# Attention and cell of a two-block model: steps half a unit apart, moving means begun behind their own tile, a narrower gate unit

## Chip, cores and metric

One NeuronCore of one Trainium2 chip runs the kernel. The metric is device time in microseconds. Five engines work beside each other, each through its own queue in program order: TensorE (PE), VectorE (DVE), ScalarE (ACT), GpSimd (POOL) and SyncE (SP), which issues the weight loads. They wait for each other by semaphores alone.

## What is computed

512 tokens of width 1024 in fp32 pass through two blocks. The first is a hybrid mixer (a state-space scan in four groups, and a pooling branch) with a feed-forward net. The second is a token mixer of sliding-window attention and a matrix-memory cell (mLSTM), again with a feed-forward net. What the change touches:

```
def causal_multiscale_pool(u, pool_w, pool_scale):
    ...
    for gi, win in enumerate(POOL_WINDOWS):            # 2, 4, 8, 16
        ...
        mean = (csg[:, 1:] - start) / jnp.minimum(count, float(win))
        outs.append(mean - u32[..., gi * gw:(gi + 1) * gw])

def token_mixer(h, w_in, ...):
    proj = h @ w_in
    qk_ml, v_ml, o_ml, gates, q_at, kv_at = jnp.split(proj, cuts, axis=-1)
    qk_ml = jax.nn.silu(causal_dwconv(qk_ml, ml_conv_w, ml_conv_b))
    ...
    h_ml = rms_norm(mlstm_chunkwise(q_ml, k_ml, v_ml, i_pre, logf), ml_norm_g) * jax.nn.sigmoid(o_ml)
    o_at = sliding_window_attention(rope(q_at), rope(k_at), v_at, attn_sinks)     # softmax with a sink
    return jnp.concatenate([h_ml, rms_norm(o_at, attn_norm_g)], axis=-1) @ w_out
```

## The kernel before

**Units.** Every weight matrix is cut into units of at most 2048 columns per partition (`plan_units`, L72). For each unit SP loads `raw` (L512), ACT rounds it to `w_hi` (`split_hi`, L1012, the activation at L1018) and POOL forms the rest, `w_lo` (`split_lo`, L553, four pieces at L561). PE then makes three products of each pair of tiles (L713 for outputs by token, L717 by channel): w_hi with the rounded activations, with their rest, and w_lo. Weights have two slots: ACT rounds the weights of the next unit at the start of a unit in its own order, so whatever ACT does at the end of the unit before stands ahead of them, and POOL and PE wait for them.

**Half units.** PE runs a unit in two halves (`project`, part 0 and 1), 24 matmuls of 512 columns each in most units. `plan_steps` (L196) gives each unit three lists of small steps: `before`, `mid` (after the first half) and `end` (after the second). Every engine walks the same lists and does its share of each step. ACT and DVE evict the tiles of a half unit ahead of its steps. `by_rank` (L191) sorts the steps of a list: those named first in `rank` (L267) come first, the rest keep their order. A slot below is one such list; slot 2n is the middle of unit n and 2n+1 its end.

**Banks.** PSUM has four banks for projections (`main`) and four for small steps, A to D. `BANKS_OF` (L275) fixes which step uses which, in order: att_scores and att_turn both use B and C, att_out D, rope_q and k_turn A, ml_scores B and C, ml_out D, B, A, C, A, C. PE may write a bank only once its last reader has freed it.

**Pooling branch.** Units U (four, two tiles each) give the pooled channels, which ACT copies to `xs_tok` (L1046). `window(t)` (DVE L1715, ACT L1242) makes tile t's moving mean by doublings, one for a window of 2 and four for 16 (L1729, L1730), corrects the first 16 tokens (L1733, L1734), scales and subtracts (L1735); ACT rounds it (L1244) and DVE forms the rest (L1738). Window 0 stands at the end of the last U unit and waits for all of its four last tiles; the others follow a half unit apart, through Y0, Y1 and the first two GS units. Units Y0, Y1 are the last group's branch, evicted by DVE (L1446), GS are gates, evicted by ACT (tanh, L1052) and DVE (L1451). DVE also adds a piece of the modulation in each (`ada_piece`, L1556).

**Second block's mixer.** Units in order: KV, QA0, QA1, GA (gates of the cell), QK (four, convolved), V0, V1, O0, O1, WO. A convolved tile (`convolve`) costs ACT L1028, then DVE three L1391, for which ACT waits, then ACT's tanh L1030; DVE's L1416 comes with the next tile. The attention runs in eight rounds q (four blocks of queries by two key heads):

- att_scores(q): PE L859, DVE L1746 to L1753 (scale, mask, maximum, sink), ACT L1262 and L1263 (exponentials)
- att_turn(q): PE transposes the probabilities (L872), ACT copies them out (L1271)
- att_out(q): PE L885, DVE L1758 to L1762; each second one also has the norm of the block, on ACT (L1283), POOL (L610, L611) and DVE (L1769)

att_scores(q) stands at the end of unit GA+q, att_turn(q) in the middle of the next and att_out(q) at its end: one round in a unit. GA has two tiles of 128 columns, 4 of them used in each, evicted with their bias by L1520. At its end stand rope_q 2 and 3 (PE L843, ACT L1254, both bank A) and ml_gates, which is one step: DVE sets rows to zero, ACT makes log-sigmoids, DVE scans them (L1780 to L1789), ACT takes exponentials (L1292 to L1295). ml_columns (PE L893, L897) needs those. k_turn(hd) needs a scaling by ACT (L1299), then PE L906 and ACT's copy L1303. The cell runs in four chunks: ml_scores(c) (PE L913, L917; DVE L1811, ACT L1309, DVE L1818 to L1824) and ml_out(c) (PE L927, L937, L943; DVE L1832 to L1856; POOL L615, L616; DVE L1867), from the end of V1 to before WO. The join multiplies by the output gate (L1874, four of them ahead of the first transposition), transposes (PE L950, L955), scales (DVE L1881), rounds (ACT L1316) and forms the rest (POOL L622); WO waits for all of it.

Of the kernel before, what the change touches and what calls it, by code (L numbers as in the profile page):

```python
# [9 lines left out]
ALU = mybir.AluOpType  # L10
# [61 lines left out]
def plan_units():  # L72
# [28 lines left out]
    u += [Unit("GA", "w_in_2", 0, KD, [(GATES2, MH, P - MH), (GATES2 + MH, MH, P - MH)], "h")]  # L101
# [94 lines left out]
def plan_steps(units):  # L196
# [39 lines left out]
    n = at["U"][3]  # L236
    for t in range(KD):
        (end, mid)[t % 2][n + (t + 1) // 2].append(("window", t))
# [28 lines left out]
    rank = ["silu", "b_turn", "ssd_out", "ssd_scores", "xs_turn", "ssd_turn"]  # L267
# [22 lines left out]
def build(nc, stream, w_ada, w_ada2, x_in, params_in, consts_in, out):  # L290
# [22 lines left out]
    with ExitStack() as ctx:  # L313
# [51 lines left out]
        with ExitStack() as s5:  # L365
# [16 lines left out]
            att = alloc(s5, "att", [32])  # L382
# [11 lines left out]
        def sem(name):  # L394
# [27 lines left out]
            ).split()]  # L422
        seg_rhs = [seg_first[:, c, :, :] for c in range(TC - 1)] + [seg_last[:, :, :]]
# [121 lines left out]
        def _(pool):  # L545
# [59 lines left out]
            def att_out(q, n):  # L605
                if q % 2 == 0:
                    return
                i = q // 2
                pool.wait_ge(at_sq, i + 1)
                link(nc.gpsimd.tensor_scalar(att[:, 26:27], att[:, 25:26], 1.0 / (AH * AD), RMS_EPS, ALU.mult, ALU.add))  # L610
                nc.gpsimd.tensor_tensor(att[:, 27:28], att[:, 26:27], small[:, 63:64], ALU.pow).then_inc(at_rs, 1)  # L611
# [13 lines left out]
            stages = {"seg_rows": seg_rows_, "ssd_scores": ssd_scores, "ssd_out": ssd_out, "att_out": att_out,  # L625
# [24 lines left out]
        def _(pe):  # L650
# [212 lines left out]
            def att_turn(q, n):  # L863
                i = q // 2
                pe.wait_ge(sm_exp, q + 1)
                for b in range(2):
                    bank, full = take(("att_turn", q), b)
                    for j in range(2):
                        for r in range(2):
                            if i == 0 and r == 0:  # L870
                                continue
                            ins = nc.tensor.transpose(bank[:, 2 * P * j + P * r:2 * P * j + P * (r + 1)],  # L872
                                                      prob[:, 2 * b + j, chunk(r)], ident)
                    ins.then_inc(full, 1)

            def att_out_(q, n):
# [4 lines left out]
                for j in range(4):  # L881
                    for r in range(2):
                        if i == 0 and r == 0:
                            continue
                        ins = nc.tensor.matmul(bank[:, AD * j:AD * (j + 1)], prob_t[:, j, r, :],  # L885
# [35 lines left out]
            def ml_out_(c, n):  # L921
# [8 lines left out]
                pe.wait_ge(v_ready, TC)  # L930
# [56 lines left out]
        def _(act):  # L987
# [44 lines left out]
            def evict(u, t):  # L1032
# [56 lines left out]
                elif u.name == "O1":  # L1089
                    bank, free = tile(j)  # L1090
                    link(run_act(og[:, t, :], bank[:, :], ACT.Tanh, scale=0.5))
# [166 lines left out]
            def att_scores(q, n):  # L1258
                ks = slice(P, 2 * P) if q < 2 else slice(0, 2 * P)
                act.wait_ge(sm_max, q + 1)  # L1260
                for j in range(4):
                    run_act(prob[:, j, ks], prob[:, j, ks], ACT.Exp, bias=att[:, 8 + j:9 + j], accum_out=att[:, 12 + j:13 + j])  # L1262
                run_act(att[:, 16:20], att[:, 16:20], ACT.Exp).then_inc(sm_exp, 1)  # L1263

            def att_turn(q, n):
                rs_ = 1 if q < 2 else 0
                if q:
                    read_by_pe(("att_out", q - 1), 0)
                for b in range(2):
                    bank, free = full(("att_turn", q), b)  # L1270
                    link(run_act(prob_t[:, 2 * b:2 * b + 2, rs_:2, :],  # L1271
# [4 lines left out]
            def att_out(q, n):  # L1276
                if q % 2:
                    i = q // 2
                    act.wait_ge(at_raw, q + 1)
                    read_by_pe(("ml_columns", 0), 0)  # L1280
                    if i:
                        act.wait_ge(at_rs, i)
# [722 lines left out]
```

## Time and profile before

| | |
|---|---|
| median of 3 runs | 1898.7 us (1897.71 to 1898.96) |
| the profiled execution | 1899.32 us, span 1897.5 us |
| mean granted clock of PE | 0.943 |
| PE matmul busy | 1704.9 us, 90% |
| PE weight loads busy | 1368.1 us, 72% |
| DVE / ACT / POOL busy | 874.3 / 637.6 / 799.2 us (46 / 34 / 42%) |
| chain that ended last, by engine | PE 70%, DVE 14%, ACT 6%, POOL 5%, issue 3% |
| HBM | 191.80 MB read, 102 GB/s over the span |

Times inside the profile count from the start of its span. Busy times say how much an engine did, and not who held up whom; for that the waits and the timelines of a stretch are read. A granted clock of 1.00 is 2.4 GHz, 0.50 is 1.2 GHz, and values between are a mean over a stretch at the two.

### The profile page before, as it was taken

Reading aid. Unit: us, or ns where it says so; the run is one execution under the profiler, and the core shown is the slowest. Engines: PE = TensorE matmul, PEld = TensorE weight load, DVE = VectorE, ACT = ScalarE, POOL = GpSimd, SP = SyncE. Lnnn points to the kernel's source line nnn. Section 1 sums busy time; section 2 is a strip of 40 time slices with the busy share of each in tenths; the row PEclk is TensorE's granted clock in tenths of the full one; section 3 lists DMA queues with packets and bytes.
Section 4 is the critical chain, followed back from the end, with each engine's and each line's share of the span. In section 5 each row is a group of like instructions: output and inputs, shape, how many; then the busy total and the mean of one; then the engine's idle time right before and its main releaser. Section 6 shows DMA issues by size and latency. Waiting matters only on the chain.

```text
span 1897.5 us, 20659 instructions
## 1 busy us (share of the span) xinstructions
PE 1704.9 (90%) x7616; PEld 1368.1 (72%) x7616; DVE 874.3 (46%) x1153; ACT 637.6 (34%) x827; POOL 799.2 (42%) x639
## 2 busy tenths in 40 slices
PE   3988999999979997999999987788869699999995
PEld 1666788787857885788888856667757377888884
DVE  5536455544484344543343455552561655203424
ACT  3534434343223223431143222443222434324331
POOL 1263555455444553455445523232134145444441
PEclk7988999999989998999999988897879799999998
DMA  8111112122324541345534531111002033232221
GB/s 308 45 67 45 67 67 89 67 89 89 122 82 166 185 177 68 131 142 185 186 136 153 178 133 48 64 50 62 23 23 71 22 130 126 76 120 89 84 92 58
DMA packets 35234, 195.22 MB, mean 103 GB/s; under 512 B 3904, under 2 KB 4032, under 8 KB 19648
## 3 DMA queue, kind: packets, MB, share of 16 engines
q1 hardware_dynamic: 23616, 151.96, 22.3%
q10 hardware_dynamic: 11520, 41.95, 6.4%
q8 instruction: 62, 1.02, 0.2%
q14 instruction: 36, 0.29, 0.0%
HBM read 191.80 MB, written 2.10 MB: 102 GB/s over the span
## 4 chain that ended last, share of the span: by engine, by line
PE 70%; DVE 14%; ACT 6%; POOL 5%; issue 3%; DMA 1%; DVEq 0%; SPq 0%; ACTq 0%; POOLq 0%
PE main L717 54%; PE main L713 8%; POOL w_lo L561 4%; ACT w_hi L1018 2%; DVE rstd L1591 1%; PE auxB L741 1%; DVE tmp L1391 1%; DVE h_lo L1621 1%; DVE tmp L1531 1%; PE auxD L820 1%; DMA ada_first<-w_ada 1%; DVE x L1606 1%; DVE ysum L1605 1%; DVE tmp L1730 1%; PE auxD L733 1%
## 5 line engine op out<-in xcount | busy, mean ns | idle before, releaser
L561 POOL TENSOR_TENSOR w_lo<-raw,w_hi 128x512 fp32r<-128x512 f32 (+1 forms) x525 | 707.6, 1379 | 903.8 <-ACT w_hi L1018 903.6
L717 PE MATMUL main<-h_hi,w_hi 128*128 128x512 f32 (+1 forms) x1144 | 460.4, 402 | 44.5 <-POOL w_lo L561 16.9
L717 PE MATMUL main<-h_lo,w_hi 128*128 128x512 f32 (+1 forms) x1144 | 451.9, 395 | 0.0
L717 PE MATMUL main<-h_hi,w_lo 128*128 128x512 f32 (+1 forms) x1144 | 451.7, 395 | 0.0
L1018 ACT ACTIVATE w_hi<-raw 128x2048 fp32r<-128x2048 f32 (+3 forms) x136 | 249.3, 1833 | 261.2 <-PE main L717 222.4
L717 PEld LDWEIGHTS main<-h_hi,w_hi 128*128 128x128 f32 (+1 forms) x1144 | 218.0, 191 | 110.1 <-issue 27.7
L717 PEld LDWEIGHTS main<-h_hi,w_lo 128*128 128x128 f32 (+1 forms) x1144 | 217.5, 190 | 48.3 <-issue 1.0
L717 PEld LDWEIGHTS main<-h_lo,w_hi 128*128 128x128 f32 (+1 forms) x1144 | 218.5, 191 | 42.9
L1531 DVE SCALAR_TENSOR_TENSOR tmp<-main,par,tmp 128x511 f32<-128x511 f32 x88 | 65.9, 749 | 176.3 <-ACT tmp L1107 174.7
L1556 DVE SCALAR_TENSOR_TENSOR ada_acc<-ada_raw,cs,ada_acc 128x1024 f32<-128x1024 f32 x70 | 115.3, 1648 | 29.2 <-DMA ada_raw<-w_ada 21.3
L713 PE MATMUL main<-w_hi,h_hi 128*128 128x512 f32 (+1 forms) x256 | 105.6, 412 | 19.8 <-POOL w_lo L561 10.2
L713 PE MATMUL main<-w_hi,h_lo 128*128 128x512 f32 (+1 forms) x256 | 101.8, 397 | 0.0
L713 PE MATMUL main<-w_lo,h_hi 128*128 128x512 f32 (+1 forms) x256 | 101.5, 397 | 0.0
L717 PE MATMUL main<-f_hi,w_hi 128*128 128x512 f32 x256 | 100.0, 391 | 0.0
L717 PE MATMUL main<-f_hi,w_lo 128*128 128x512 f32 x256 | 99.7, 389 | 0.0
L717 PE MATMUL main<-f_lo,w_hi 128*128 128x512 f32 x256 | 99.6, 389 | 0.0
L1391 DVE SCALAR_TENSOR_TENSOR tmp<-main,half,tmp 128x511 f32<-128x511 f32 (+2 forms) x96 | 71.9, 748 | 48.0 <-ACT tmp L1028 45.5
L713 PEld LDWEIGHTS main<-w_hi,h_hi 128*128 128x128 f32 x256 | 52.0, 203 | 33.9 <-POOL w_lo L561 11.0
L717 PE MATMUL main<-g_hi,w_hi 128*128 128x512 f32 x176 | 68.7, 390 | 0.8 <-POOL w_lo L561 0.8
L717 PE MATMUL main<-g_lo,w_hi 128*128 128x512 f32 x176 | 68.5, 389 | 0.0
L717 PE MATMUL main<-g_hi,w_lo 128*128 128x512 f32 x176 | 68.5, 389 | 0.0
L1485 DVE TENSOR_TENSOR tmp<-tmp 128x512 f32<-128x512 f32 x32 | 24.7, 771 | 93.5 <-ACT f_hi L1079 93.5
(329 smaller groups left out, 2390.8 us busy)
## 6 DMA issues: line engine op xcount, KB each, us to landing
raw<-stream SPq DMA_DIRECT2D x119, 1024.0 KB, 4.9
ada_raw<-w_ada ACTq DMA_DIRECT2D x80, 512.0 KB, 4.2
ada_first<-w_ada SPq DMA_DIRECT2D x16, 512.0 KB, 6.8
raw<-stream SPq DMA_DIRECT2D x8, 768.0 KB, 4.1
raw<-stream SPq DMA_DIRECT2D x8, 640.0 KB, 3.8
x<-x_in SPq DMA_DIRECT2D x2, 2048.0 KB, 10.6
out<-x SPq DMA_DIRECT2D x8, 256.0 KB, 2.0
con<-consts SPq DMA_DIRECT2D x1, 486.0 KB, 3.7
```

What stands on the lines that cost most here:

```text
L561: ins = nc.gpsimd.tensor_tensor(w_lo[:, s, a:b], raw[:, s, a:b], w_hi[:, s, a:b], ALU.subtract)
L713: ins = nc.tensor.matmul(bank[:, 0:u.cols], a[:, ka_, chunk(t)], w[:, k, :], start=start, stop=stop)
L717: ins = nc.tensor.matmul(bank[0:n, :], w[:, k, col:col + n], a[:, ka_, :], start=start, stop=stop)
L733: ins = nc.tensor.matmul(aux["D"][:, :], ones, tmp[:, k % 2, :], start=(k == 0), stop=(k == KD - 1))
L741: ins = nc.tensor.matmul(bank[:, t:t + 1], acc[:, chunk(t)], ones[:, 0:1], start=True, stop=True)
L820: ins = nc.tensor.matmul(bank[:, HD * k:HD * (k + 1)], decay[:, k, :], xdt[:, 0, HD * k:HD * (k + 1)], start=True, stop=True)
L1018: run_act(w_hi[:, s, 0:k], raw[:, s, 0:k], ACT.Copy).then_inc(hi_done, 1)
L1391: ins = stt(acc[:, d:SEQ], bank[:, 0:SEQ - d], w[:, 3 - d:4 - d], acc[:, d:SEQ], ALU.mult, ALU.add)
L1485: link(tt(tmp[:, 2 + n % 2, :], tmp[:, n % 2, :], tmp[:, n % 2, :], ALU.mult))
L1531: link(stt(acc[:, d:SEQ], bank[:, 0:SEQ - d], wt, acc[:, d:SEQ], ALU.mult, ALU.add))
L1556: link(stt(acc, src, c, acc, ALU.mult, ALU.add))
L1591: link(nc.vector.reciprocal(rstd[:, :], rstd[:, :]))
```

## The change

- Windows of the pooling branch: window t moves to slot 2·U[2]+t, and DVE waits for its own tile alone.
- GA packs both gates into one tile of 36 columns; DVE copies the two groups of rows out, frees the bank and adds the biases after.
- ml_gates is cut into three steps (ml_gates, ml_scan, ml_exp) at the end of GA, the middle of QK0 and its end.
- Attention: one round in each half unit from the middle of QK0: scores in slot s, turn in s+2, output in s+3. `prob` and `prob_t` get a second buffer each, which lies in `og`, and `att` has four slots. The block norm becomes the steps att_square and att_norm.
- k_turn starts half a unit earlier; ml_scores and ml_out stand half a unit apart, from the middle of V1; v_ready is awaited chunk by chunk.
- The join multiplies each chunk by its gate just before that chunk is transposed.
- `rank` is longer.

```diff
-    u += [Unit("GA", "w_in_2", 0, KD, [(GATES2, MH, P - MH), (GATES2 + MH, MH, P - MH)], "h")]
+    u += [Unit("GA", "w_in_2", 0, KD, [(GATES2, MH, 32 - MH), (GATES2 + MH, MH, 0)], "h")]
...
-    n = at["U"][3]
     for t in range(KD):
-        (end, mid)[t % 2][n + (t + 1) // 2].append(("window", t))
+        slot(2 * at["U"][2] + t).append(("window", t))
...
-    mid[at["GA"][0]] += [("rope_q", 0), ("rope_q", 1)]
-    end[at["GA"][0]] += [("rope_q", 2), ("rope_q", 3), ("ml_gates", 0)]
+    end[at["GA"][0]] += [("rope_q", 0), ("rope_q", 1), ("ml_gates", 0)]
+    mid[at["QK"][0]] += [("rope_q", 2), ("rope_q", 3), ("ml_scan", 0)]
+    end[at["QK"][0]] += [("ml_exp", 0)]
     mid[at["QK"][1]] += [("ml_columns", 0)]
     for hd in range(MH):
-        (end, mid)[hd % 2][at["QK"][3] + (hd + 1) // 2].append(("k_turn", hd))
-    n = at["GA"][0]
+        slot(2 * at["QK"][3] + hd).append(("k_turn", hd))
+    first = 2 * at["QK"][0]
     for q in range(2 * TC):
-        end[n + q + 1].append(("att_out", q))
-    for q in range(2 * TC):
-        mid[n + q + 1].append(("att_turn", q))
-        end[n + q].append(("att_scores", q))
-    end[at["V1"][0]] += [("ml_scores", 0)]
-    mid[at["O0"][0]] += [("ml_out", 0), ("ml_scores", 1)]
-    end[at["O0"][0]] += [("ml_out", 1), ("ml_scores", 2)]
-    mid[at["O1"][0]] += [("ml_out", 2), ("ml_scores", 3)]
-    before[at["WO"][0]] += [("ml_out", 3)] + [("join", c) for c in range(TC)]
+        slot(first + q).append(("att_scores", q))
+        slot(first + q + 2).append(("att_turn", q))
+        slot(first + q + 3).append(("att_out", q))
+    for i in range(TC):
+        slot(first + 2 * i + 5).append(("att_square", i))
+        slot(first + 2 * i + 6).append(("att_norm", i))
+    for c in range(TC):
+        slot(2 * at["V1"][0] + c).append(("ml_scores", c))
+        slot(2 * at["V1"][0] + c + 1).append(("ml_out", c))
+    before[at["WO"][0]] += [("join", c) for c in range(TC)]
...
-    rank = ["silu", "b_turn", "ssd_out", "ssd_scores", "xs_turn", "ssd_turn"]
+    rank = ["silu", "b_turn", "ssd_out", "ssd_scores", "xs_turn", "ssd_turn", "rope_q", "ml_columns", "att_turn", "att_out",
+            "att_scores", "k_turn", "ml_out", "ml_scores"]
...
+        probs = [prob[:, :, :], og[:, 0:2, :].rearrange("p a (j k) -> p (a j) k", k=2 * P)]
+        probs_t = [prob_t[:, :, :, :], og[:, 2:4, :].rearrange("p a (j r k) -> p (a j) r k", r=2, k=P)]
...
-                pe.wait_ge(v_ready, TC)
+                pe.wait_ge(v_ready, c + 1)
...
             def att_turn(q, n):
                 rs_ = 1 if q < 2 else 0
-                if q:
-                    read_by_pe(("att_out", q - 1), 0)
+                if q >= 2:
+                    read_by_pe(("att_out", q - 2), 0)
...
-                    link(ts((row_i, row_f)[t], bank[0:MH, :], pc("gate_b", t, t + 1)[0:MH, :], None, ALU.add))
+                    nc.vector.tensor_copy(row_i, bank[0:MH, :])
+                    link(nc.vector.tensor_copy(row_f, bank[32:32 + MH, :]))
                     dve.sem_inc(free, 1)
+                    ts(row_i, row_i, pc("gate_b", 0, 1)[0:MH, :], None, ALU.add)
+                    link(ts(row_f, row_f, pc("gate_b", 1, 2)[0:MH, :], None, ALU.add))
...
             def window(t, n):
...
-                if t == 0:
-
-                    j = units[unit_at["U"][3]].job0 + 1
-                    for b in range(4):
-                        dve.wait_ge(main_free[(j - b) % 4], (j - b) // 4 + 1)
-                else:
+                j = units[unit_at["U"][t // 2]].job0 + t % 2
+                dve.wait_ge(main_free[j % 4], j // 4 + 1)
+                if t:
                     dve.wait_ge(pl_lo, t)
...
-                    for k in range(TC):
-                        stt(hm[:, k, :], og[:, k, :], 1.0, hm[:, k, :], ALU.add, ALU.mult).then_inc(ml_out, 1)
+                stt(hm[:, c, :], og[:, c, :], 1.0, hm[:, c, :], ALU.add, ALU.mult).then_inc(ml_out, 1)
```

## Rows read from the trace of the kernel before

**Rows 1.** Windows: us, PE, PEld, DVE, ACT, POOL busy (x), PEclk, DMA share, GB/s.
```profile
528.80:579.90 51.10, 38.03 (x148) 30.41 (x147) 38.41 (x60) 11.10 (x13) 22.34 (x14) 0.87 0.27 93
...
1203.20:1291.40 88.20, 69.55 (x314) 56.67 (x313) 45.00 (x90) 39.74 (x80) 21.69 (x20) 0.86 0.14 48
1291.40:1403.40 112.00, 96.10 (x486) 79.56 (x486) 49.73 (x115) 32.78 (x70) 25.88 (x26) 0.90 0.11 38
```

**Rows 2.** Waits of PE, 505 to 580 us: total, times, longest.
```profile
PE main L717 <- POOL w_lo L561: 13.1, 3, 5.7
```

**Rows 3.** Waits of PE, 1187 to 1426 us.
```profile
PE auxB L872 <- ACT att L1263: 13.5, 3, 8.9
PE auxA L906 <- ACTq L1300: 9.0, 3, 5.0
```

**Rows 4.** Timeline of POOL near 525 us: start, length, instruction, idle before.
```profile
526.70 6.55 POOL L561 TENSOR_TENSOR w_lo<-raw,w_hi 128x512 fp32r<-128x512 f32 x4 [9.76 <-ACT w_hi L1018]
```

**Rows 5.** Timeline of DVE, windows 0 and 1 (507 to 519 us).
```profile
507.08 0.15 DVE L1729 COPY tmp<-xs_tok 128x1 f32<-128x1 f32 x1 [16.52 <-ACT xs_tok L1046]
507.15 0.68 DVE L1730 TENSOR_TENSOR tmp<-xs_tok 128x511 f32<-128x511 f32 x1
...
509.59 0.69 DVE L1738 TENSOR_TENSOR p_lo<-tmp,p_hi 128x512 fp32r<-128x512 f32 x1 [0.76 <-ACT p_hi L1244]
...
512.72 1.81 DVE L1730 TENSOR_TENSOR tmp<-xs_tok 128x511 f32<-128x511 f32 x1
...
518.31 0.69 DVE L1738 TENSOR_TENSOR p_lo<-tmp,p_hi 128x512 fp32r<-128x512 f32 x1 [0.76 <-ACT p_hi L1244]
```

**Rows 6.** Timeline of POOL, w_lo of QK0.
```profile
1189.73 5.15 POOL L561 TENSOR_TENSOR w_lo<-raw,w_hi 128x512 fp32r<-128x512 f32 x4 [5.75 <-ACT w_hi L1018]
```

**Rows 7.** Timeline of DVE, ml_gates' scans up to the first scores.
```profile
1207.74 0.68 DVE L1780 SCALAR_TENSOR_TENSOR k_tok<-k_tok,v 4x512 f32<-4x512 f32 x1 [4.73 <-ACT v L1290]
...
1213.79 0.40 DVE L1746 SCALAR_TENSOR_TENSOR prob<-auxB,con 128x256 f32<-128x256 f32 x1
```

**Rows 8.** Timeline of ACT, 1251 to 1261 us: exponentials, a convolution, the turned copies.
```profile
1251.48 0.51 ACT L1262 ACTIVATE prob<-prob,att 128x256 f32<-128x256 f32 x1 [4.99 <-DVE att L1753]
...
1253.55 1.90 ACT L1018 ACTIVATE w_hi<-raw 128x2048 fp32r<-128x2048 f32 x1
1255.35 0.76 ACT L1028 ACTIVATE tmp<-main,half 128x512 f32<-128x512 f32 x1
1258.55 0.63 ACT L1030 ACTIVATE tmp<-tmp 128x512 f32<-128x512 f32 x1 [2.44 <-DVEq L1395]
...
1259.86 0.60 ACT L1271 ACTIVATE prob_t<-auxC 128x512 f32<-128x512 f32 x1 [0.18 <-ACT prob_t L1271]
```

**Rows 9.** Chain that ended last, 1250 to 1560 us: two half units and WO.
```profile
1300.35 5.49 PE main L713 x24
...
1337.86 7.55 PE main L713 x24
...
1424.95 46.45 PE main L717 x192
```

**Rows 10.** Score matmuls of one bank: timeline near 1264, groups of 1282 to 1292.
```profile
1264.20 1.02 PE L859 MATMUL auxC<-ka,qa 64*128 64x256 f32 x4
...
L859 PE MATMUL auxC<-ka,qa 64*128 64x256 f32 x4 | 1.9, 631 | 0.0
```

**Rows 11.** Timeline of DVE, one round's scores: first and last instruction.
```profile
1248.07 0.69 DVE L1746 SCALAR_TENSOR_TENSOR prob<-auxB,con 128x512 f32<-128x512 f32 x1 [0.15 <-DVE qa L1769]
...
1251.29 0.15 DVE L1753 TENSOR_TENSOR att<-par,att 128x4 f32<-128x4 f32 x1
```

**Rows 12.** Timeline of DVE, ml_out and ml_scores of one slot: first and last.
```profile
1383.27 0.43 DVE L1832 TENSOR_TENSOR tmp<-auxA,qcol 128x258 f32<-128x258 f32 x1 [3.48 <-PE auxD L937]
...
1395.06 0.70 DVE L1824 TENSOR_TENSOR tmp<-v,qcol 128x516 f32<-128x516 f32 x1 [0.25 <-DVE tmp L1819]
```

**Rows 13.** Groups of POOL, 1414 to 1425 us.
```profile
L622 POOL TENSOR_TENSOR h_lo<-tmp,h_hi 128x512 fp32r<-128x512 f32 x8 | 9.9, 1273 | 4.8 <-ACT h_hi L1316 4.8
```

More of the change, by code:

```diff
@@ L381, in build @@
             dec = alloc(s5, "dec", [MH * TC])
-            att = alloc(s5, "att", [32])
+            att = alloc(s5, "att", [4, 32])
             decb = alloc(s5, "decb", [MH * TC])
@@ L603, in ssd_out, with att_square @@
                 nc.gpsimd.tensor_tensor(ss[:, 2:3], ss[:, 1:2], small[:, 63:64], ALU.pow).then_inc(y_rs, 1)
[L605 to L608, printed above, removed]
+            def att_square(i, n):
+                st = att[:, i % 4, :]
                 pool.wait_ge(at_sq, i + 1)
[L610 to L611 removed]
+                link(nc.gpsimd.tensor_scalar(st[:, 26:27], st[:, 25:26], 1.0 / (AH * AD), RMS_EPS, ALU.mult, ALU.add))
+                nc.gpsimd.tensor_tensor(st[:, 27:28], st[:, 26:27], small[:, 63:64], ALU.pow).then_inc(at_rs, 1)
             def ml_out_(c, n):
@@ L1090, in evict @@
                     bank, free = tile(j)
+                    if t == 0:
+                        read_by_pe(("att_out", 2 * TC - 1), 0)
                     link(run_act(og[:, t, :], bank[:, :], ACT.Tanh, scale=0.5))
@@ L1274, in att_turn, with att_square @@
                     act.sem_inc(pt_ready, 1)
[L1276 to L1282, printed above, removed]
-                    run_act(quant[:, :], qa[:, i, :, :].rearrange("p t d -> p (t d)"), ACT.Square,
-                            accum_out=att[:, 25:26]).then_inc(at_sq, 1)
+            def att_square(i, n):
+                act.wait_ge(at_raw, 2 * i + 2)
+                read_by_pe(("ml_columns", 0), 0)
+                run_act(quant[:, :], qa[:, i, :, :].rearrange("p t d -> p (t d)"), ACT.Square,
+                        accum_out=att[:, i % 4, 25:26]).then_inc(at_sq, 1)
             def ml_gates(i, n):
@@ L1290, in ml_gates, with ml_exp @@
                 run_act(row_e, row_e, ACT.Ln, bias=ones[0:MH, 0:1]).then_inc(mg_e, 1)
+            def ml_exp(i, n):
                 act.wait_ge(mg_x, 2)
@@ L1320, in _ @@
                       "b_turn": b_turn, "ssd_scores": ssd_scores, "ssd_norm": ssd_norm, "ssd_out": ssd_out, "ssd_turn": ssd_turn, "window": window,
-                      "rope_k": rope_k, "rope_q": rope_q, "att_scores": att_scores, "att_turn": att_turn, "att_out": att_out,
-                      "ml_gates": ml_gates, "k_turn": k_turn, "ml_scores": ml_scores, "join": join}
+                      "rope_k": rope_k, "rope_q": rope_q, "att_scores": att_scores, "att_turn": att_turn, "att_square": att_square,
+                      "ml_gates": ml_gates, "ml_exp": ml_exp, "k_turn": k_turn, "ml_scores": ml_scores, "join": join}
             count = {}
@@ L1742, in att_scores @@
                 ks = slice(P, 2 * P) if q < 2 else slice(0, 2 * P)
-                kn = ks.stop - ks.start
+                pr, st = probs[q % 2], att[:, q % 4, :]
+                if q >= 2:
+                    full(("att_turn", q - 2), 1)
                 for b in range(2):
                     bank, free = full(("att_scores", q), b)
-                    ins = stt(prob[:, 2 * b:2 * b + 2, ks], bank[:, :].rearrange("p (j k) -> p j k", j=2)[:, :, ks],
+                    ins = stt(pr[:, 2 * b:2 * b + 2, ks], bank[:, :].rearrange("p (j k) -> p j k", j=2)[:, :, ks],
                               float(AD) ** -0.5, each(cc("band", ks.start, ks.stop), 2), ALU.mult, ALU.add)
@@ L1777, in ml_gates, with ml_scan @@
                 dve.sem_inc(mg_x, 1)
+            def ml_scan(i, n):
+                scan = nc.vector.tensor_tensor_scan
                 dve.wait_ge(mg_e, 1)
@@ L1889, in _ @@
                       "ssd_scores": ssd_scores, "ssd_out": ssd_out, "ssd_turn": ssd_turn, "window": window,
-                      "att_scores": att_scores, "att_out": att_out, "ml_gates": ml_gates, "ml_columns": ml_columns,
+                      "att_scores": att_scores, "att_out": att_out, "att_norm": att_norm, "ml_gates": ml_gates,
+                      "ml_scan": ml_scan, "ml_columns": ml_columns,
                       "ml_scores": ml_scores, "ml_out": ml_out_, "join": join}
```

41 lines of the change are left out of this document (21 added, 20 removed).

## The prediction

> **What bounds the kernel now.** I read the tables by stretch first. In the windows of the pooling branch PE was busy 38.03 of 51.1 us; in the attention stretch (1203.2 to 1291.4) 69.55 of 88.2, in the stretch of the cell 96.10 of 112.0, at mean granted clocks of 0.87, 0.86 and 0.90 [rows 1]. Elsewhere PE is nearly full, so what the change can win lies in these stretches. The waits of PE say who ends them: in the first, w_lo of the next unit's weights, 13.1 us in 3 waits [rows 2]; in the others, L872 on the exponentials of ACT (13.5 us, the longest 8.9) and L906 on k_turn's scaling (9.0 us in 3) [rows 3]. The timelines of ACT and DVE then show why these are late: both run in program order, and each waits inside a step for the other.
>
> The bound that a measurement can tell from no change is 0.2%, 3.8 us. I sum against the profiled run (1899.32 us, of which 1.8 us lie outside its 1897.5 us span) and take the difference off the median of 1898.7, 0.6 us lower.
>
> **Windows of the pooling branch.** No instruction is added; three of four waits before the first window go, and windows 0 to 7 move three half units earlier. What hurts now: ACT's p_hi copy waits for each window, and w_hi of the next unit stands behind it. w_lo of GS0, held by it, ran from 526.70 to 533.25, and GS0 began then instead of at 528.8, where its stretch begins [rows 1, 4]. A window with two taps took 3.1 us on DVE (507.08 to 510.2), and 6.3 (512.7 to 519.0) where POOL ran w_lo beside it [rows 5]. Each doubling adds what the first one took, 507.08 to 507.83, 0.8 us: 3.1, 3.9, 4.7, 5.5 alone, and some 2.5 more beside w_lo (between nothing and the 3.2 of [rows 5]; I lean to the upper). Placed by DVE's own order: windows 0 to 3 fall at 487 to 508, where DVE was idle 16.52 us [rows 5], with w_lo for Y0 ready at 504 and for Y1 at 515, no stall. Window 4 starts at 512.7 (after Y0's second tile) and lasts to 519, the ada piece and two evictions to 521.6, window 5's copy on ACT ends at 525.7, w_hi (1.9) at 528, w_lo (6.5, beside window 6) at 534.1: a stall of 5.4 where 4.5 stood. Window 6 runs 527.8 to 535.9; window 7 starts at 538.5 and its copy ends at 543.1; w_hi 545.3, w_lo 550.4, against GS0's end at 546.7: a stall of 3.8. Then ACT is free, and the third stall (5.7) is gone. GS0 to GS2 took 51.1 - 13.1 = 38.0 us, 12.7 each [rows 1, 2]; GS0 and GS1 keep that, GS2 behind no stall gets two main blocks of 5.49, 11.0 [rows 9]: it ends at 574.1 instead of 579.9. **Gain 5.8 us**, from 2 (every window beside w_lo) to 9 (none).
>
> **Gate unit GA.** Its 256 padded columns become 36, one job of 24 matmuls instead of two: 5.5 us of PE go (one main block, 5.49 [rows 9]). Its weight load, w_hi and w_lo shrink in proportion. The two added copies and the separate adds on DVE (two more instructions on four partitions) lie under w_lo of QK0, which ends at 1194.88 [rows 6]. QK0 can start then, since rope_q 2, 3 and the first scores leave this spot too: 8.3 us ahead of 1203.2, where the attention stretch begins in before.
>
> **The first half units.** ml_scan's 6.05 us on DVE (1207.74 to 1213.79 [rows 7]) no longer hold up the first exponentials, the cause of the 8.9 us wait. But rope_q 2 and 3 now stand in QK0's middle, and share bank A: rope_q 3 needs ACT's copy of 2, behind ml_gates, w_hi and the whole convolution. DVE copies, adds and zeroes until 1197.4; ACT's part takes the 4.7 us for which DVE waited [rows 7], then w_hi and the convolution: 1202.0, 1203.9, 1207.7. PE, done at 1200.5, waits to 1208.5, does rope_q 3 and the scores and QK0's second half at the slow block's pace: 1217.9. ml_exp ends at 1228.0, ml_columns waits 3.1 us for it (QK1's first half ends at 1224.9), and the half unit after that, with a second wait for the copies, ends at 1244.2.
>
> **The steady half unit.** Before, a unit held one score step; now a half unit does, and att_turn(q-2) and att_scores(q) stand in the same slot, both with banks B and C. PE can't write scores before ACT has copied the turned probabilities out, and ACT does that after its convolution, in which it waits for DVE. From the start C of L1028: L1030 at C+3.2, bank C copied out at C+5.1, B at C+4.4 (1255.35, 1258.55, 1260.46 [rows 8]). Score matmuls 2.0 (1.02 for one bank [rows 10]), main block 5.5 or 5.6: C' = C + 12.0 at full clock. ACT's own path is close: scores full at C+6.4, DVE 3.4 us from the first L1746 to the end of L1753 [rows 11], of which 2.9 follow the second bank, four exponentials and L1263 2.1 us (1251.48 to the w_hi at 1253.55 [rows 8]), together C+11.5, and every second slot w_hi 1.9 [rows 8]. What the clock costs is unknown: nothing (L859 at 1.02 us), or 0.9 on each bank (1.9 instead of 1.02 [rows 10]) and 2.1 on the main block (5.49 to 7.55 [rows 9]), 3.9 in all. In the attention stretch the mean clock of 0.86 over 88.2 us is 24.7 us at the lower level, 12.3 lost over eight half units: I take 1.4, nearest to that row, and 2.3 to 2.5 in the three half units with a second wait. So 13.4 each: 1257.7, 1271.2, 1284.6 for the ends of QK2 and QK3's first half.
>
> In QK3's two middle slots k_turn stands last: PE waits for L1299, behind the exponentials, 5.7 us each. They end at 1306.5 and, with V0's first half, 1327.3. V0 and V1 have no convolution, the turned tiles are copied at once, and a half unit takes some 4.1 (turn, output and k_turn, an estimate by the 2.0 of the scores) + 5.6: 1337.0, 1346.7, 1356.4. There ml_out starts, with no attention left beside it.
>
> **Cell.** DVE needs 12.5 us from the first L1832 to the end of L1824 [rows 12], and PE's L927 and L937 ahead of it some 1.5 (estimate): 14.0 a half unit. Ends: 1370.4, 1384.4, 1398.4. The last ml_out (5.0) now lies before O1's second half, which ends at 1409.8. The join then starts after the tanh of the last output tile; one L1874 instead of four precedes the first L1881, and POOL's eight L622, 9.9 us [rows 13], set the end: 0.7 + 0.7 + 0.7 + 0.8 + 0.6 + 9.9 and gaps, 14.0. WO begins at 1423.8, before at 1424.95 [rows 9]. **Gain 1.1 us**, between a gain of 16 (no clock loss at all) and a loss of 14 (the full 3.9 in each attention slot, 2 in each cell slot).
>
> The four st slots in att, the use of og as second buffers and the finer v_ready waits cost nothing: the gate tanh of O1 starts two units after the last att_out.
>
> **Sum.** 5.8 + 1.1 = 6.9 us; 1898.7 - 6.9 = **1891.8 us**.
>
> **Rivals.**
> (a) The clock stays up: PE's waits in the new slots are 1.5 to 3 us, shorter than the 8.9 and 5.0 of before [rows 3]. Then attention gains about 13 and the total is 1880. For it: the stretch of the cell, all small steps and short waits, had the higher clock, 0.90 [rows 1]. Against it: each slot has three small steps and a wait in a row. Chance 0.26.
> (b) Slower: the new slot keeps the clock at its lower level. Its place is the score step of QK1 to V0: small matmuls, the wait for bank B, small matmuls, main block. Price, from [rows 9, 10]: 3.9 instead of 1.4 to 2.5 in seven slots, some +14, and 2 more in each later slot that the lower clock reaches, up to +20: 1898.7 - 5.8 + 13 to 19, about 1909 with part of it. It decides from about 11 us more than I count. For it: a mean clock of 0.86 already with half as many steps. Chance 0.2.
> (c) The windows gain nothing: w_lo of GS0 is late by more than 1 us beyond my 534.1 and drags GS1 and GS2. Then 1897 to 1899, no change. The mechanism is the meeting of windows and w_lo: L561's four parts took 6.55 us beside a window against 5.15 [rows 4, 6], and DVE's L1730 took 1.81 instead of 0.68 [rows 5]. Windows 4 and 6 start beside a w_lo. Each further 1.3 us that a window waits (a fourth of 5.15) passes by ACT into the next w_lo; four of them use up the gain, and the total is 1897. Chance 0.2. The Trainium skill (SBUF — State Buffer, SBUF: two separate sides) says that such a VectorE instruction and a GpSimd instruction take a shared port in turn, each for its whole length. The trace agrees (1.81 us [rows 5]); taken strictly it would make every SBUF instruction of windows 4, 6 and half of 7 wait, which is this rival's 1897, and not the 1891.8 of the sum.
> (d) The forecast, within 1886 to 1896: 0.34.
>
> **Numbers.** Faster by over 3.8 us: (a) and most of (d), 0.57. Within: (c) and the rest of (d), 0.22. Slower: (b) with a little of (c), 0.21. The range takes in (a) and most of (b): 1879 to 1906.
>
> **What would show it.** Right: no wait of PE on w_lo before GS0, and two in place of three after it; new waits of PE at L859 on ACT's L1271, of 1.5 to 3 us; L906 waiting 5 to 6 us twice; QK1 to QK3 longer than before, O0 and O1 shorter; WO starting 1 us earlier in the stretch alone. Wrong: half units of 10 us or less in QK2 (then the ACT chain isn't the limit), or of 16 (the clock), or PE waiting for w_lo in QK or V.

## The result, and the profile after

The changed kernel takes **1903.4 us** (median of 15 runs, 1900.3 to 1904.5) against 1898.9 us for the kernel before (15 runs, 1897.7 to 1901.7): a ratio of 1.002, 95% interval 1.0013 to 1.0027. It is slower by about 4 us, where I forecast 1891.8. Its profiled execution took 1904.53 us (before 1899.32), with a span of 1902.7 us (before 1897.5) and a mean granted clock of 0.939 (before 0.943).

First the table by stretch, with the bounds of [rows 1]: length, busy time and count of PE, PEld, DVE, ACT and POOL, then the granted clock.

```profile
528.80:579.90 51.10, 39.39 (x156) 31.59 (x155) 26.40 (x36) 10.47 (x12) 24.28 (x16) 0.87 0.32 107
1203.20:1291.40 88.20, 69.04 (x248) 53.85 (x249) 42.56 (x87) 30.86 (x76) 15.30 (x12) 0.71 0.11 36
1291.40:1403.40 112.00, 90.62 (x494) 76.17 (x493) 50.61 (x113) 34.72 (x69) 27.11 (x30) 0.91 0.11 38
```

In the second stretch PE was busy as long as before (69.04 against 69.55 us), but issued 248 matmuls instead of 314, at 0.71 of full clock instead of 0.86 [rows 1]. This is the row that a reader should stop at. The steps have moved, so the same bounds hold in part other work; but where the busy time stays while the count of matmuls and the granted clock both fall, the matmuls run slower.

Next PE's waits, between 480 and 580 us (the first row), and between 1190 and 1431 us.

```profile
PE main L719 <- POOL w_lo L565: 13.1, 3, 6.3
...
PE auxB L861 <- ACTq L1278: 15.3, 6, 3.3
PE auxA L908 <- ACTq L1303: 11.6, 4, 5.5
PE auxA L845 <- ACTq L1259: 7.8, 2, 7.1
PE auxA L957 <- DVE hm L1881: 7.7, 4, 3.4
PE auxC L919 <- DVEq L1854: 3.2, 3, 1.3
PE main L719 <- POOL h_lo L624: 3.1, 1, 3.1
PE auxA L895 <- ACT quant L1298: 3.0, 1, 3.0
```

Lines have shifted: L861 is the scores of attention, L1278 the release of a bank after ACT's copy of the turned probabilities, L908 and L1303 k_turn, L845 and L1259 rope_q, L957 the join's transposition of a chunk. The waits on w_lo in the windows add up to the same 13.1 us as before [rows 2]. The waits on the exponentials [rows 3] are gone, and in their place stands a new wait for bank B in six half units.

One half unit of QK2 as TensorE's timeline shows it, and the main blocks from the chain that ended last:

```profile
1251.00 2.04 PE L861 MATMUL auxB<-ka,qa 64*128 64x256 f32 x4 [3.14 <-ACTq L1278]
1252.84 1.91 PE L861 MATMUL auxC<-ka,qa 64*128 64x256 f32 x4
...
1211.40 7.83 PE main L719 x24
1238.81 7.79 PE main L719 x24
1254.75 8.31 PE main L719 x24
1271.83 8.32 PE main L719 x24
...
1430.89 45.44 PE main L719 x192
```

A wait of 3.14 us, score matmuls at 2.04 and 1.91 us (1.02 at full clock [rows 10]), then a main block of 8.3 us where 5.49 is the full-clock length [rows 9]. WO starts at 1430.89, 5.9 us later than before [rows 9]; the span is 5.2 us longer.

My half units beside the measured ones (ends of their main blocks, us):

| | forecast | measured | late by |
|---|---|---|---|
| wait for rope_q 3 | 1208.5 | 1208.3 | -0.2 |
| QK0, second half | 1217.9 | 1219.2 | 1.3 |
| QK1, second half | 1244.2 | 1246.6 | 2.4 |
| QK2 | 1257.7, 1271.2 | 1263.0, 1280.1 | 5.3, 8.9 |
| QK3, first half | 1284.6 | 1295.4 | 10.8 |
| V0, first half | 1327.3 | 1336.4 | 9.1 |
| V1 | 1356.4 | 1363.8 | 7.4 |
| O1 | 1398.4, 1409.8 | 1403.1, 1412.9 | 4.7, 3.1 |
| WO starts | 1423.8 | 1430.9 | 7.1 |

The forecast times in this table stand on the clock of the trace before and leave out the windows' gain of 5.8 us, which I summed apart.

### The profile page after: what moved, and what is told of

The parts are those of the page before. It is cut to its first block, busy times and chain, and to the rows that moved or that the text cites. A ratio compares the mean times of both kernels' runs of the same rounds, so it can differ in the third digit from the quotient of the medians.

```text
span 1902.7 us, 20619 instructions
## 1 busy us (share of the span) xinstructions
PE 1704.0 (90%) x7592; PEld 1364.5 (72%) x7592; DVE 873.8 (46%) x1155; ACT 636.1 (33%) x827; POOL 796.2 (42%) x636
## 3 DMA queue, kind: packets, MB, share of 16 engines
q8 instruction: 62, 1.02, 0.2%
## 4 chain that ended last, share of the span: by engine, by line
PE 72%; DVE 13%; ACT 5%; POOL 5%; issue 3%; DMA 1%; DVEq 0%; SPq 0%; ACTq 0%; POOLq 0%
PE main L719 56%; PE main L715 8%; POOL w_lo L565 4%; ACT w_hi L1020 2%; DVE rstd L1597 1%; DVE tmp L1394 1%; PE auxB L743 1%; DVE h_lo L1627 1%; DVE tmp L1537 1%; PE auxD L822 1%; DMA ada_first<-w_ada 1%; PE auxD L735 1%; PE auxB L861 1%; DVE x L1612 1%; DVE ysum L1611 1%
## 5 line engine op out<-in xcount | busy, mean ns | idle before, releaser
L719 PE MATMUL main<-h_hi,w_hi 128*128 128x512 f32 (+2 forms) x1136 | 461.4, 406 | 41.3 <-DVE h_lo L1627 16.4
L719 PE MATMUL main<-h_lo,w_hi 128*128 128x512 f32 (+2 forms) x1136 | 452.9, 399 | 0.0
L719 PE MATMUL main<-h_hi,w_lo 128*128 128x512 f32 (+2 forms) x1136 | 451.9, 398 | 0.0
L719 PEld LDWEIGHTS main<-h_hi,w_hi 128*128 128x128 f32 (+2 forms) x1136 | 218.2, 192 | 109.7 <-issue 27.9
L719 PEld LDWEIGHTS main<-h_hi,w_lo 128*128 128x128 f32 (+2 forms) x1136 | 218.0, 192 | 49.6 <-issue 1.0
L719 PEld LDWEIGHTS main<-h_lo,w_hi 128*128 128x128 f32 (+2 forms) x1136 | 218.6, 192 | 44.0
L715 PE MATMUL main<-w_hi,h_hi 128*128 128x512 f32 (+1 forms) x256 | 102.0, 399 | 19.8 <-POOL w_lo L565 10.2
```

What stands on the lines that cost most here:

```text
L715: ins = nc.tensor.matmul(bank[:, 0:u.cols], a[:, ka_, chunk(t)], w[:, k, :], start=start, stop=stop)
L719: ins = nc.tensor.matmul(bank[0:n, :], w[:, k, col:col + n], a[:, ka_, :], start=start, stop=stop)
```

## The parts of the change, one at a time

The time of each kernel below is a median, and its ratio is against runs of the kernel before on the same chip. The kernels below ran on four chips; the medians of the kernel before lie between 1899.2 and 1899.9 us there and at 1898.9 above, so differences between kernels of different chips are good to about 1 us.

**Windows alone** (the kernel before with the new start of the windows):

```diff
-        (end, mid)[t % 2][n + (t + 1) // 2].append(("window", t))
+        slot(2 * at["U"][2] + t).append(("window", t))
...
```

> The kernel before with the new start of the windows alone; attention, gate unit and cell as before. Theory (the trace after: w_lo still 13.1 us late in 3 waits, GS2 ends 0.4 us earlier): the same time as before, 1898 to 1899, a difference of at most 1 us; PE's waits on w_lo before GS0 and GS1 of about 6.3 and 5.4 us. Rival, the prediction's own term: 5.8 us faster, 1893, with the longest wait under 5.5. A second rival, that the earlier windows only help once the attention is not there to shift the clock, would also show here as over 2 us faster.

Measured: 1899.5 us, ratio 0.9996 (0.9987 to 1.0005). The windows' part is worth nothing: by the interval at most 2.5 us, and PE's waits on w_lo are the expected ones (13.2 us in 3, the longest 6.3). ACT and POOL of the changed kernel show why, and DVE's small copies beside POOL:

```profile
509.41 0.63 ACT L1248 ACTIVATE p_hi<-tmp 128x512 fp32r<-128x512 f32 x1 [2.90 <-DVEq L1739]
...
526.67 0.63 ACT L1248 ACTIVATE p_hi<-tmp 128x512 fp32r<-128x512 f32 x1 [6.70 <-DVEq L1739]
...
527.21 1.90 ACT L1020 ACTIVATE w_hi<-raw 128x2048 fp32r<-128x2048 f32 x1
...
529.18 7.02 POOL L565 TENSOR_TENSOR w_lo<-raw,w_hi 128x512 fp32r<-128x512 f32 x4 [10.76 <-ACT w_hi L1020]
...
529.92 1.11 DVE L1732 COPY tmp<-tmp 128x2 f32<-128x2 f32 x1
...
542.59 0.17 DVE L1732 COPY tmp<-tmp 128x4 f32<-128x4 f32 x1
```

The chain is window, p_hi, w_hi, w_lo, PE, as before. A copy of a few columns takes 1.11 us beside w_lo and 0.17 without it. Window 4 lasted 8.6 us (512.1 to 520.7) beside Y1's w_lo, window 6 9.3 us, where windows 5 and 7, with POOL idle, took 4.8 and 5.6 us; w_lo itself took 7.02 us. The 3.8 us are four instructions of each window at 0.9 to 1.0 us more. In window 6 these are the three copies on `tmp` and the first correction of 16 columns (L1736, 1.12 instead of 0.17), while each long addition of a doubling kept its 0.68.

**All without the windows** (the kernel after with their old start):

> The kernel after with the windows started as before. Theory: the whole loss stands in attention, cell and join, so 1903 to 1904, 4.5 to 5.5 us slower than before, and within 1 us of after. Rival: the earlier windows cost something that the span hides; then this one is faster than after by over 1 us.

Measured: 1902.3 us, ratio 1.001 (1.0002 to 1.0019). The ratio is 0.1% under that of the kernel after, within the interval: the loss stands in attention, cell and join. Its 12 runs lie between 1896.3 and 1904.1, wider than the others; the last section comes back to this.

**The narrow gate unit alone:**

```diff
-    [(GATES2, MH, P - MH), (GATES2 + MH, MH, P - MH)]
+    [(GATES2, MH, 32 - MH), (GATES2 + MH, MH, 0)]
...
```

> The kernel before with the gate unit of 36 columns in place of 256, and nothing else. Theory: one main block of 5.5 us less on TensorE, behind which nothing waits: 1893 to 1894, 5 to 5.5 us faster. Rival: TensorE then only meets the wait on the exponentials (8.9 us before) earlier, since that wait ends by VectorE's scans and not by TensorE; then 0 to 2 us faster, with that wait grown to about 14 us.

Measured: 1897.8 us, ratio 0.9995 (0.9986 to 1.0003), so 1.7 us by the medians and nothing beyond doubt. The rival holds in its time, but not in its figure: the wait on the exponentials, at most 8.9 us before [rows 3], grew to 10.6 and not to 14. A wait for rope_q's copy took in 1.4 us more (2.16 us instead of 0.73), and these exponentials themselves ended 1.5 us earlier.

```profile
PE auxB L872 <- ACT att L1263: 15.2, 3, 10.6
```

**The join's gate multiplications first** (the kernel after, the four in a row again):

```diff
                     finish_heads()
-                stt(hm[:, c, :], og[:, c, :], 1.0, hm[:, c, :], ALU.add, ALU.mult).then_inc(ml_out, 1)
+                    for k in range(TC):
+                        stt(hm[:, k, :], og[:, k, :], 1.0, hm[:, k, :], ALU.add, ALU.mult).then_inc(ml_out, 1)
```

> The kernel after with the join's four gate multiplications ahead of its first transposition, as before. Theory: in the join TensorE, VectorE and GpSimd go round once per chunk since the multiplication of the next chunk comes behind the two evictions of this one (3.3 us a chunk, GpSimd idle 0.36 us in each); with the four first, 2.1 us go ahead of the first transposition and each chunk falls to GpSimd's 2.5 to 2.9 us: join 17 to 18 us, the total within 1 us of after. Rival: the ping-pong is all of the join's excess over my 14.0 us: 3 to 4 us faster than after, 1900.

Measured: 1904.4 us, ratio 1.0026 (1.0015 to 1.0037), against 1.002 for the kernel after: no change in the total. Theory and rival had differed in just this, and the total is the theory's. The join itself, from the last main block of O1 to WO, went from 18.0 to 16.0 us; in this execution a main block of O1 took 8.51 us where the kernel after had 5.78, which hides it. Of the rival's 3 to 4 us there are 2. The groups of POOL in the join, first of the kernel after, then of this one:

```profile
L624 POOL TENSOR_TENSOR h_lo<-tmp,h_hi 128x512 fp32r<-128x512 f32 x8 | 11.2, 1400 | 4.4 <-ACT h_hi L1319 4.1
```

```profile
L624 POOL TENSOR_TENSOR h_lo<-tmp,h_hi 128x512 fp32r<-128x512 f32 x8 | 9.9, 1263 | 4.8 <-ACT h_hi L1319 4.8
```

With the multiplications between the evictions POOL's eight subtractions take 1400 ns each instead of 1263, and it idles 0.36 us before each pair. With them first its 9.9 us are back [rows 13].

## What sets a half unit of attention

**Filler.** If the excess of QK2's half units is the clock, matmuls that keep TensorE busy in its waits must shorten them:

```diff
                 pe.wait_ge(ka_ready, 1)
+                if 3 <= q <= 6:
+                    pe.wait_ge(aux_free["A"], bank_use["ml_columns", 0][0][1] + 1)
+                    for _ in range(12):
+                        nc.tensor.matmul(aux["A"][:, :], h_hi[:, 0, 0:P], h_hi[:, 1, :], start=True, stop=True)
```

> The kernel after with 12 matmuls of 128 by 512 whose result nobody reads (h_hi against h_hi, into bank A) on TensorE in each of four half units of the attention (q 3 to 6), where it waits for bank B; 12 times 0.23 us is 2.8 us, less than the 3.1 us wait, so at an unchanged clock they cost nothing. Theory (the clock is the excess of these slots): the score matmuls after them take 1.02 us instead of 2.04 and the main block 5.5 to 6 instead of 8.4, so the slots of QK2 fall from 16.5 and 17.1 us to 12.5 to 13.5, and the total by 8 to 14 us to 1890 to 1896. Rival (the slots are set by the ping-pong of ScalarE and VectorE): slots stay at 16 us, total 1903 to 1905.

Measured: **1891.8 us**, ratio 0.9962 (0.9949 to 0.9974), 11.5 us under the kernel after by more work. The stretch of q 3 to 5 in the kernel after (first) and here: length, busy time of PE, clock.

```profile
1247.86:1295.40 47.54, 39.05 (x139) 0.71 0.07 23
```

```profile
1248.22:1285.00 36.78, 35.80 (x176) 1.00 0.08 29
...
1251.27 1.13 PE L865 MATMUL auxB<-ka,qa 64*128 64x256 f32 x4 [0.23 <-ACTq L1282]
1252.24 1.02 PE L865 MATMUL auxC<-ka,qa 64*128 64x256 f32 x4
```

The three half units took 12.0, 12.9 and 13.0 us instead of 16.5, 17.1 and 15.2; the main blocks 5.74 to 5.77 instead of 8.36, 8.37 and 6.93. My C + 12.0 at full clock was right in the first of them; the clock adds 4.4 us to QK2's first half (1.8 on the scores, 2.6 on the main block).

**The copies first.** The bank is late because ACT copies it after its convolution, in which it waits for DVE. Here `early` picks att_turn out of the steps of a QK unit and `rest` leaves the others, in both halves of the unit:

```diff
+                run(early(mid[u.n]))
                 if u.last:
                     for t in range(u.n_jobs // 2):
                         evict(u, t)
-                run(sorted(mid[u.n], key=act_order))
+                run(sorted(rest(mid[u.n]), key=act_order))
...
```

> The kernel after with ScalarE's two copies of the turned probabilities ahead of its convolution in each half unit of QK, so that banks B and C come free while TensorE still does the output step. Theory: the wait for bank B (15.3 us in 6 on L1278) falls under 4 us in all, and with it some of the clock; slots of 13 to 14 us, total 8 to 12 us under after, 1892 to 1896. Rival: ScalarE only hands its own delay on, since its convolution, its exponentials and w_hi then start 2.7 us later in each slot: the wait moves to the turn step (on the exponentials) or to w_lo, and the total stays within 2 us of after.

Measured: 1893.6 us, ratio 0.9966 (0.9953 to 0.9978), 9.8 us under the kernel after. The profiled execution was the fastest of the five, 1890.6 us.

```profile
PE auxA L908 <- ACTq L1303: 17.7, 4, 8.5
PE auxA L845 <- ACTq L1259: 7.8, 2, 7.1
...
PE auxB L861 <- ACTq L1278: 6.1, 3, 3.4
```

The wait for bank B fell from 15.3 to 6.1 us, not under 4; the half units of QK2 and QK3's first took 8.9, 15.6 and 10.2 us instead of 16.5, 17.1 and 15.2. Part of the rival is seen too: k_turn's two long waits grew from 5.5 to 8.5 us, since ACT comes to the scaling of k later.

**k scaled one half unit ahead** (a step k_scale, whose only part is ACT's L1300 to L1302):

```diff
         slot(2 * at["QK"][3] + hd).append(("k_turn", hd))
+        slot(2 * at["QK"][3] + hd - 1).append(("k_scale", hd))
...
```

> The kernel after with ScalarE's scaling of k one half unit ahead of the transposition that reads it. Theory: the two waits of 5.5 us on L1303 (11.6 us in 4) fall under 2 us each; the two slots get 3.5 to 5.5 us shorter each, but the copies and exponentials behind them are then the limit, so 5 to 9 us faster than after, 1895 to 1898. Rival: TensorE waits as long in the next slot for the same exponentials: no change.

Measured: 1893.9 us, ratio 0.9969 (0.9957 to 0.9981), 9.5 us under the kernel after, where 5 to 9 were expected. The waits on L1303 are gone, and only the wait for bank B grows a little:

```profile
PE auxB L862 <- ACTq L1279: 16.1, 6, 3.3
PE auxA L846 <- ACTq L1260: 7.8, 2, 7.1
```

**w_hi ahead of the window's copy** at the end of U2, U3, Y0, Y1, GS0 and GS1:

```diff
+                if u.n in ahead:
+                    split_hi(units[u.n + 2])
                 run(sorted(end[u.n], key=act_order))
...
```

> The kernel after with w_hi of the unit after next on ScalarE ahead of the window's copy that stands at a unit's end (U2 to GS1). Theory (w_hi stands behind the copy of a window, and w_lo behind w_hi): w_lo is there before its unit, TensorE's three waits of 1.4, 6.3 and 5.4 us go, and the total falls by 9 to 13 us to 1890 to 1894. Rival: w_lo and the windows then meet all the time on GpSimd and VectorE, the windows themselves get late and PE waits in PW for the last one: 3 to 6 us faster at most.

Measured: 1894.5 us, ratio 0.9974 (0.9963 to 0.9986), 8.8 us under the kernel after, just short of the 9 to 13 expected. Waits of PE in the windows:

```profile
PE main L719 <- DVE x L1452: 4.2, 2, 3.0
PE main L719 <- POOL w_lo L565: 2.6, 2, 2.0
```

6.8 us instead of 13.1, and GS2 ends at 572.1 instead of 579.5. What is late now is DVE: the evictions of Y0 and Y1 stand behind a window.

## Together

Copies first, k ahead, w_hi ahead and the join's multiplications first (called c1 below):

> The kernel after with four edits together: the turn copies first on ScalarE, k scaled one half unit ahead, w_hi ahead of the window's copy, the four gate multiplications of the join first. Theory (each takes a wait of its own, and the 8.5 us waits on L1303 that the first edit alone left are taken by the second): the gains of 9.7, 9.5 and 8.8 us add up, and 0 to 2 us of the join: 1873 to 1877. Rival: the first two share the exponentials as one limit and add up to 12 only: 1880 to 1884.

Measured: **1865.1 us**, ratio 0.9817 (0.9801 to 0.9832), 38 us under the kernel after, 8 us below the best that I had expected; the single gains add up to 28. I take it that copies first and k ahead need each other (the 8.5 us waits), but no run has these two alone. Two half units in a row, without and with a wait for bank B:

```profile
1236.27:1245.16 8.89, 8.89 (x47) 1.00 0.01 2
1245.16:1262.42 17.26, 13.78 (x51) 0.70 0.17 61
```

Filler in place of the copies first, the rest as there:

> The kernel after with the filler matmuls, k scaled ahead, w_hi ahead and the gate multiplications first. Theory: the filler keeps the clock in q 3 to 6, the scaled k takes the two 5.5 us waits, 11.5 + 9.5 + 8.8 us: 1871 to 1876; half units of 12 to 13 us up to QK3. Rival: the two last slots (q 7 and V0) fall back to the lower clock without filler, and half of the third gain goes: 1877 to 1881.

Measured: 1873.8 us, ratio 0.9860 (0.9846 to 0.9874), as expected (1871 to 1876).

The kernel before, its attention and cell in the old order, with the new windows, the narrow gate unit, k ahead and w_hi ahead:

> The kernel before, its attention and cell in the old order, with the earlier windows, the narrow gate unit, k scaled ahead and w_hi ahead. Theory (the half-unit order is what makes room): 1.7 us by the gate unit, 7 to 9 by w_hi, and 5 to 8 by the k scaling (9.0 us of waits in 3): 1882 to 1886, 8 us or more above c1. Rival: the old order is as good once the same waits are gone: within 3 us of c1, 1873 to 1878; then the new order itself brings nothing.

Measured: 1875.1 us, ratio 0.9868 (0.9854 to 0.9881): the rival's time, but 10 us above c1, so neither had it whole. With the copies last, the new order needs filler to be as good as the old one (1873.8 against 1875.1 us); with the copies first it is 10 us ahead. The old order was not run with its copies first, nor with filler, so how much of the 10 us is the order's own stays open.

c1 with two banks for rope_q, and ml_columns half a unit later:

```diff
+        elif name == "rope_q":
+            banks = "AD"[item % 2]
...
-    mid[at["QK"][1]] += [("ml_columns", 0)]
+    end[at["QK"][1]] += [("ml_columns", 0)]
```

> c1 with rope_q alternating between banks A and D, so that rope_q 3 need not wait for the copy of rope_q 2, and ml_columns one half unit later. Theory (L845 waited 7.1 us for that copy and nothing else needed it so early): the 7.1 us wait and the 3.0 us wait on L1298 go, part of it comes back as a wait on ScalarE's first exponentials: 4 to 7 us below c1, 1868 to 1871. Rival: the first scores then wait as long for ScalarE, whose convolution, gates and exponentials are the limit of these slots: within 1 us of c1.

Measured: 1871.8 us, ratio 0.9851 (0.9837 to 0.9864): 6.7 us **slower** than c1, against both theories. Waits of PE from 1186 to 1300 us, c1 first:

```profile
PE auxA L846 <- ACTq L1260: 7.8, 2, 7.1
PE auxB L862 <- ACTq L1279: 7.1, 3, 3.5
PE auxA L896 <- ACT quant L1299: 3.0, 1, 3.0
```

```profile
PE auxB L864 <- ACTq L1281: 10.2, 4, 6.8
PE auxD L890 <- DVEq L1818: 5.5, 1, 5.5
PE auxB L877 <- DVEq L1766: 4.2, 1, 4.2
PE main L722 <- POOL w_lo L568: 0.9, 1, 0.9
```

The waits of 17.9 us became 20.8. That is the 2.7 us between the two profiled executions (1871.6 against 1868.9 us, c1's slowest); the rest of the 6.7 us by the medians no profile shows. As I read the rows, the 7.1 us for rope_q's copy were cover for ACT's and DVE's scans, convolutions and exponentials; without it TensorE meets these (4.2 us for DVE's reading of bank B, 6.8 for ACT's copy of it). And ml_columns, moved behind the turn of q 1 and beside an output step on the same bank D, made the new 5.5 us wait on DVE's copy of it. Which of the two edits costs more wasn't tried apart.

**Filler in all waits**, on the kernel after (26 in front of rope_q 3, 11 in front of ml_columns, and q 3 to 6), and on c1 (the same with q 4 and q 6):

```diff
+                if c == 3:
+                    filler("D", 26)
                 bank, full = take(("rope_q", c), 0)
...
```

> The kernel after with filler matmuls of 128 by 512 in the 7.1 us wait of rope_q 3 (26 into bank D), in the 3.0 us wait of ml_columns (11), and in q 3 to 6 as before. Theory (a wait of 3 us or more lowers the clock for what follows, small steps alone don't): QK0's second half has a main block of 5.7 us instead of 7.9, the scores of q 0 take 2.0 instead of 2.3; q 2, with its own wait of 2.5 us left, is helped in part; 2 to 6 us below the filler in q 3 to 6 alone, 1886 to 1890. Rival (the limit of these slots is ScalarE's chain): PE gets to the same waits earlier and waits longer, the total stays at 1891 to 1893.

Measured: 1895.9 us, ratio 0.9979 (0.9970 to 0.9988), 3 to 4 us worse than filler in q 3 to 6 alone. QK0's second main block did fall from 7.89 to 5.75 us, so the low clock there does come from the long wait. But TensorE then waited as long in other places: 2.4 us for ml_exp behind the 2.7 us of filler (3.0 us without), and 3.9 us at q 2 instead of 2.4. The chain of ACT and DVE ends these half units: the rival's mechanism holds, though the total missed its 1891 to 1893 as well. By the profiled executions this kernel was still 3.4 us ahead at the end of QK3's first half, and 0.6 us behind at the start of WO: a block of QK3 and one of O1 took 8.13 and 8.59 us instead of 6.87 and 5.73. Why the clock was lower there stays open.

> c1 with the same filler in the waits of rope_q 3 and ml_columns, and 12 matmuls ahead of the scores of q 4 and q 6, where it waited 3.4 us each. Theory: the score step falls from 3.95 to 2.15 us and the main block from 8.4 and 7.6 to 5.7 behind each, the first two half units give 2 to 4 us more: 8 to 13 us below c1, 1852 to 1857. Rival: in c1 every second half unit has no wait at all (it took 8.9 us), so ScalarE's chain over two half units is the limit; a faster TensorE then waits longer in the next: 2 to 4 us below c1.

Measured: **1861.4 us**, ratio 0.9797 (0.9783 to 0.9810), the fastest here: 3.7 us under c1 by the medians, the rival's figure again; the two intervals overlap, so that the two kernels differ is likely and not shown. The two half units with filler have full clock (main blocks of 5.74 and 5.72 us), and the one between now waits 1.5 us where it waited none, with a main block of 7.45 us instead of 5.73: the filler moved the low clock on.

## Why the prediction was wrong, by its own steps

- **Where the loss is.** The forecast was 12 us too low. By the profiled executions: 5.8 us of windows that didn't come, 7.1 us by the start of WO, 0.7 back after it. Three terms of the sum failed: the windows' gain, the clock in the steady half unit, and the join.
- **Windows, gain 5.8: rival (c), and this step failed.** The order of steps and the place of the stalls were right (6.3 and 5.4 us, forecast 5.4 and 3.8), and so were the windows without w_lo beside them (4.8 and 5.6 us for 4.7 and 5.5). Beside w_lo they took 3.8 us more, and I had taken 2.5 with 3.2 as the end; w_lo of GS0 took 7.02 where I had 6.5 and ended at 536.2, 2.1 us behind my 534.1, where (c) asks for more than 1. A third stall of 1.4 us stood before Y1, where I had written none: windows 0 and 2 met a w_lo too, window 3 ended at 510.8 and not by 508, and its p_hi came at 509.4. GS2 took 10.9 us for my 11.0, but GS0 and GS1 took 13.0 and 14.0 for 12.6 and 12.7. The term that I left out is that short instructions on DVE, of 2 to 16 columns, wait 0.9 to 1.0 us too: I had priced the doubling by its long addition.
- **Gate unit, 5.5 us.** Right in place (QK0 at 1195.0, forecast 1194.9). That it is worth little alone, since the exponentials end later than TensorE, I had counted in the new order, as PE's 8 us up to rope_q 3, whose wait ended within 0.2 us of my time.
- **The steady half unit.** The mechanism, bank B behind ACT's convolution, and its 12.0 us at full clock were right. **The clock term failed**: 1.4 us taken, 2.9 and 3.6 us short in QK2's two half units by the table, 8.4 us by the end of QK3's first half; filler gives them back. The mean of the old order (0.86) was the wrong row to lean on: there the scores had no wait ahead of them, and the waits stood ahead of the turn. One of 3.71 us was followed by a main block of 6.25 us, where 3.14 us in the new half unit, between output and scores, are followed by slow scores and a block of 8.36. This was rival (b). Its price of 3.9 was nearly right (4.4 in QK2's first half), but three half units alone paid it in full, QK1's second and QK2's two (main blocks of 7.8 to 8.4 us); the next three, up to V0's first, paid in part (blocks of 6.9 to 7.0). Why a half unit with turn, output, wait and scores in a row gets the lower clock is argued from these rows; that it is the clock, the filler shows.
- **k_turn's waits.** 5.5 us twice, forecast 5.7.
- **V and cell.** 9.0 us a half unit for 9.7, and 13.1 for 14.0: my estimates for small matmuls were too high. With 1.4 us in QK3's second half they gave back 7.7 us.
- **Join, 14.0 us: mis-sized.** It took 18.0. The last chunk's heads were scaled only 2.2 us after O1's end, where I had it start behind the tanh, after 0.7: DVE's part of the last ml_out (1405.0 to 1413.6) and POOL's root behind it (to 1415.1) ended only then. And POOL's 9.9 us became 12.6 by the gate multiplication in each chunk. With the multiplications first, 2 us of it came back.
- **Rival (a)**, the clock staying up, is what filler makes: 1891.8 us, not 1880. The windows' 5.8 us and the join's 4.0 are still missing there, and QK0's and QK1's second main blocks still took 7.7 us. That 1891.8 is also my forecast is chance.
- What I said would show it: L861's waits of 1.5 to 3 us (2.0 to 3.3) and L908's two of 5 to 6 us came; half units of 16 us in QK2 were named as the sign of the clock, and came; a wait on w_lo before Y1 I had excluded.

## What to carry to other kernels

An engine that copies a bank out should do it ahead of any step in which it waits for another engine; here the finer interleaving paid only with it or with filler (1865 us with all edits, against 1875 for the old order without the copies first), and cost 4 us as it was. Price a new short wait with small matmuls around it at the lower clock for all that follows, up to the end of the next block, and test that with filler before anything is rearranged. Before a wait is taken away, ask what ends next: the gate unit's 5.5 us brought 1.7, no more than the noise, and taking away the 7.1 us wait for rope_q's copy, together with a later ml_columns, made the kernel slower.

## What the hardware showed that I had not expected

Twelve matmuls of 0.25 us whose result nobody reads, in each of four waits of 2.0 to 3.3 us, made the kernel 11.5 us faster; the granted clock went from 0.71 to 1.00 over the same three half units. The Trainium skill (TensorE: Matmul & The Clock Gate, A second HAM failure mode: psum-queue depth-cycling) says of another kernel that short idle times between groups of matmuls, over and over, sent the clock back and forth between its levels. The trace agrees: 0.71 is a mean over three half units, between the two levels.

What the lower clock costs may differ from one execution to the next. The attention of the kernel without the new windows is the same code as after, and its profiled execution (1897.8 us, the median is 1902.3) had main blocks of 7.09, 8.08 and 6.79 us in the places where after had 8.36, 8.37 and 6.93, at a clock of 0.81 instead of 0.71. The times of its runs, 1896.3 to 1904.1, are not explained by that: the mean clock of these runs was 0.939 to 0.941, and no lower where they took longer. With the copies first it did fall with the time, from 0.942 (1890.6 us) to 0.938 (1894.9 us). What spreads the runs stays open; a difference of a few us can't be read from one profile.

The meeting of DVE and POOL costs both: a copy of a few columns 1.11 instead of 0.17 us, w_lo up to 7.02 us instead of 5.15 [rows 6].
